# Expert rows scattered plainly into a table and fetched twice near the end, instead of accumulated into the token rows by DMA

## The reference

```python
def moe_swiglu(h, w_router, w1, w3, w2):
    logits = (h @ w_router).astype(jnp.float32)
    top_val, top_idx = lax.top_k(logits, TOP_K)          # TOP_K = 2
    top_w = jax.nn.softmax(top_val, axis=-1)
    combine = jnp.sum(jax.nn.one_hot(top_idx, N_EXPERTS, dtype=jnp.float32) * top_w[..., None], axis=-2)
    out = jnp.zeros_like(h)
    for e in range(N_EXPERTS):
        out = out + combine[..., e:e + 1].astype(h.dtype) * swiglu(h, w1[e], w3[e], w2[e])
    return out
...
x = x + moe_swiglu(h, moe_router[i], moe_w1[i], moe_w3[i], moe_w2[i])
...
return rms_norm(x, final_g)
```

## Time and profile before

| | us |
|---|---|
| median of 3 runs | 1800.87 (1799.14 to 1803.2) |
| the profiled execution | 1802.62 |
| its span, first to last instruction | 1800.9 |

### The profile page before, as it was taken

One profiled execution on the slowest core, in us unless ns is written; L12 is line 12 of the kernel. 1 busy time (PEld: TensorE's weight loads), 2 busy tenths in 40 slices (PEclk: granted clock), 3 DMA queues, 4 the chain that ended last, 5 costly groups with the idle time before them and its releaser, 6 DMA issues.

```text
span 1800.9 us, 24793 instructions
## 1 busy us (share of the span) xinstructions
PE 1778.0 (99%) x10058; PEld 1525.1 (85%) x10058; DVE 1507.2 (84%) x1402; ACT 1207.6 (67%) x1135; POOL 85.8 (5%) x97
## 2 busy tenths in 40 slices
PE   9999999999999999999999999999999999999997
PEld 9989898899999989898888887877878777787775
DVE  7999866566557999876579898999989899998997
ACT  5657754454445557654576787878878787787785
POOL 1000000100001000000100001001010010000000
PEclk9999999999999999999999999999999999999999
DMA  8444555345554544454468999999999999999995
GB/s 342 180 172 142 186 187 187 118 164 210 186 182 158 193 177 141 169 223 169 154 229 315 417 427 407 426 427 420 427 402 428 425 423 421 406 426 425 416 415 222
DMA packets 55826, 519.87 MB, mean 289 GB/s; under 512 B 7136, under 2 KB 7392, under 8 KB 12320
## 3 DMA queue, kind: packets, MB, share of 16 engines
q1 hardware_dynamic: 52448, 507.83, 70.7%
q0 software_dynamic: 2544, 9.18, 1.7%
q10 hardware_dynamic: 720, 1.31, 0.2%
HBM read 511.74 MB, written 6.55 MB: 288 GB/s over the span
## 4 chain that ended last, share of the span: by engine, by line
PE 84%; DVE 10%; ACT 4%; issue 2%; DMA 1%; SPq 0%; ACTq 0%; DVEq 0%
PE psum L2140 15%; PE psum L2126 13%; PE psum L2128 13%; PE psum L2127 13%; PE psum L2141 8%; PE psum L2634 7%; PE psum L2635 7%; DVE raw_alias L1374 3%; DVE U_alias L1374 2%; DVE wlo L1374 2%; ACT whi L832 1%; PE psum L2647 1%; PE psum L2629 1%; PE psum L2653 1%; ACT wlo L832 1%
## 5 line engine op out<-in xcount | busy, mean ns | idle before, releaser
L832 ACT ACTIVATE whi<-raw 128x2048 fp32r<-128x2048 f32 (+1 forms) x225 | 424.0, 1896 | 68.9 <-PE psum L2141 50.0
L1374 DVE TENSOR_TENSOR wlo<-raw,whi 128x2048 fp32r<-128x2048 f32 (+1 forms) x144 | 326.3, 2267 | 131.6 <-ACT whi L832 131.3
L2140 PE MATMUL psum<-h_hl,whi 128*128 128x512 f32 x1216 | 430.6, 398 | 0.3 <-DVE U L1732 0.2
L2141 PE MATMUL psum<-h_hl,wlo 128*128 128x256 f32 x1216 | 340.4, 280 | 0.0
L2140 PEld LDWEIGHTS psum<-h_hl,whi 128*128 128x128 f32 x1216 | 228.2, 188 | 55.4 <-issue 1.2
L2141 PEld LDWEIGHTS psum<-h_hl,wlo 128*128 128x128 f32 x1216 | 229.5, 189 | 0.1
L1374 DVE TENSOR_TENSOR raw_alias<-raw,wlo 128x2048 fp32r<-128x2048 f32 x87 | 196.5, 2284 | 18.4 <-ACT wlo L832 18.2
L2126 PE MATMUL psum<-act_hl,whi 128*128 128x256 f32 x720 | 206.1, 286 | 0.9 <-DVE wlo L1374 0.5
L2127 PE MATMUL psum<-act_hl,whi 128*128 128x256 f32 x720 | 203.7, 283 | 0.0
L2128 PE MATMUL psum<-act_hl,wlo 128*128 128x256 f32 x720 | 203.6, 283 | 0.0
L1374 DVE TENSOR_TENSOR raw_alias<-raw,whi 128x2048 fp32r<-128x2048 f32 x81 | 183.4, 2285 | 13.6 <-ACT whi L832 13.5
(11 more groups left out here) (335 smaller groups left out, 3379.4 us busy)
## 6 DMA issues: line engine op xcount, KB each, us to landing
raw<-in_stream SPq DMA_DIRECT2D x87, 2048.0 KB, 15.5
raw<-in_stream SPq DMA_DIRECT2D x141, 1024.0 KB, 4.8
U<-in_stream SPq DMA_DIRECT2D x52, 2048.0 KB, 14.2
memhat<-in_stream SPq DMA_DIRECT2D x29, 1024.0 KB, 11.1
h_hl_alias<-in_stream SPq DMA_DIRECT2D x29, 1024.0 KB, 13.1
raw<-in_stream SPq DMA_DIRECT2D x6, 512.0 KB, 3.7
xacc<-U POOLq DMA_DIRECT2D x3, 512.0 KB, 8.0
xT<-in_x_cols ACTq DMA_DIRECT2D x4, 256.0 KB, 6.9
```

Of the source, the lines that this page charges most:

```text
L832: act.activation(hi_home(n)[:, first:words], src[:, first:words], ACT.Copy).then_inc(hi_ready, 1)
L1374: dve.tensor_tensor(lo_home(n)[:, first:words], src[:, first:words], hi_home(n)[:, first:words].bitcast(F32), ALU.subtract).then_inc(lo_re ...
L2140: pe.matmul(o[:].rearrange("p (a b) -> p a b", a=2), st[0], mv, start=start, stop=False)
L2141: return pe.matmul(o[:, 0:256], st[1], mv[:, 0, :], start=False, stop=stop)
```

## The change

- `xacc` is replaced by `ys`: a row of zeros and 128 rows for each of the first 7 experts. Each expert's rows are stored into their own place by a plain scatter, with no addition. Rows of empty slots are dropped by a bounds check (an index beyond the table), in the scatters and in the gathers of tokens.
- `ys` is filled once, by 7 DMAs that ACT issues in layer 1 beside chunks 30 to 36 of its mixer and one for the zero row.
- DVE makes a list of where each token's two rows lie (`rows_listed`, at n = 16), as a larger and a smaller index. POOL fetches the rows of the smaller index into `xa` ahead of the scatter of p = 6, and those of the larger index into `xsum` after it.
- The residual: `xrows` and `x_rows` leave the opening steps, and the stores `kept` with them. PE transposes only the first block of tokens, after step 53, and DVE adds it to `xa` at n = 325 and 326. The second block is added by PE itself into the final sums, by 4 matmuls of `xT` with the identity in each of `final_rows(2)` and `(3)`.
- DVE adds `xsum` to `xa` in four pieces: at n = 333, 334, 335, and after the last split. `final_rows` wait for that; they move behind `turned(STEPS - 1)` and between the last down parts.
- A few expert's tokens are fetched as half rows on all 128 partitions.
- The shares are read in place (`wslot`), without the copy to `wcur`.

The diff, cut to its core:

```diff
@@ gpsimd
-            gp.iota(spare, ...)
-            gp.iota(minus_spare, ...)
+            gp.iota(row_of, pattern=[[SLOTS, NE]], base=1 + FAR, channel_multiplier=1, ...)
+            gp.memset(half_of, float(2 * S)).then_inc(rt_const, 1)
...
-            def kept(t):
-                gp.wait_ge(xt_ready, 2 * t + 2)
-                gp.dma_start(xacc[P * t:P * t + P, :], xtok).then_inc(scr_in, 16)
-            kept(0)
             gp.wait_ge(ix_ready, 1)
...
-                gp.indirect_dma_start(out=hg[0:there, :], out_offset=None, in_=hrow,
-                                      in_offset=bass.IndirectOffsetOnAxis(ap=gidx[0:there, p:p + 1], axis=0))\
-                  .then_inc(hg_in, 16)
-            for e in range(NE):
-                if e:
+                if few(p):
+                    out, rows, last = hg[:, 0:D // 2], hrow.rearrange("s (h d) -> (s h) d", h=2), 2 * S - 1
+                else:
+                    out, rows, last = hg, hrow, S - 1
+                gp.indirect_dma_start(out=out, out_offset=None, in_=rows,
+                                      in_offset=bass.IndirectOffsetOnAxis(ap=gidx[:, p:p + 1], axis=0),
+                                      bounds_check=last, oob_is_err=False).then_inc(hg_in, 16)
+            def sums_in(to, first):
+                for b in range(TB):
+                    at = first + b
+                    gp.indirect_dma_start(out=to[:, b, :], out_offset=None, in_=ys,
+                                          in_offset=bass.IndirectOffsetOnAxis(ap=yidx[:, at:at + 1], axis=0)).then_inc(xa_in, 16)
+            rows_in(1)
+            rows_in(2)
+            gp.wait_ge(scr_in, 16 * NE)
+            for e in range(NE - 1):
+                if e == NE - 2:
                     gp.wait_ge(y_sent, sent(e))
-                gp.tensor_copy(wcur, wslot[:, e:e + 1]).then_inc(wc_ready, 1)
...
-                    gp.indirect_dma_start(out=xacc, ..., in_=y[0:here, :], in_offset=None, compute_op=ALU.add)
-            gp.wait_ge(ga_done, NE)
-            gp.dma_start(xa, xacc[0:S, :].rearrange("(b p) d -> p b d", p=P)).then_inc(xa_in, 16)
+                    gp.wait_ge(ga_done, NE)
+                    sums_in(xa, TB)
+                here = HALF if few(e) else SLOTS
+                gp.wait_ge(y_ev, e + 2)
+                gp.indirect_dma_start(out=ys, ..., in_=y[0:here, :], in_offset=None,
+                                      bounds_check=(NE - 1) * SLOTS, oob_is_err=False).then_inc(y_sent, 16)
+                if e + 3 < NE:
+                    rows_in(e + 3)
+            gp.wait_ge(y_sent, sent(NE - 1))
+            sums_in(xsum, 0)
@@ scalar
+                    p = n - BASE[1] - CLEARED          # CLEARED = 30
+                    if 0 <= p < NE - 1:
+                        act.dma_start(ys[1 + SLOTS * p:1 + SLOTS * p + SLOTS, :].rearrange("p (a b) -> p a b", a=DB),
+                                      ones[:].unsqueeze(1).to_broadcast([P, DB, P])).then_inc(scr_in, 16)
...
             token_rows()
-            x_rows(0)
+            act.wait_ge(y_ev, 1)
+            act.dma_start(ys[0:1, :], y[0:1, :]).then_inc(scr_in, 16)
...
                 act.wait_ge(w_used, MOE + down_end(ENDS[p]) + 1)
-                act.wait_ge(wc_ready, p + 1)
+                if p:
+                    act.wait_ge(y_sent, sent(p))
...
                 for n in range(SPLIT, TOTAL):
-                    if n in (9, 15, 27):
-                        x_rows({9: 1, 15: 2, 27: 3}[n])
...
-                act.wait_ge(wc_ready, NE)
+                act.wait_ge(xa_sum, TB + 2)
@@ vector
+            def rows_listed():
+                ... (5 elementwise instructions and 2 reductions of 14 numbers per partition, a difference, a copy)
+            def kept_added(i):
+                t, at = i // 2, slice(512 * (i % 2), 512 * (i % 2) + 512)
+                if i == 0:
+                    dve.wait_ge(xa_in, 16 * TB)
+                dve.wait_ge(xt_done, i + 1)
+                dve.tensor_tensor(xa[:, t, at], bank[4 + i][:], xa[:, t, at], ALU.add).then_inc(xt_ready, 1)
+            def halves_added(i):
+                t, at = i // 2, slice(512 * (i % 2), 512 * (i % 2) + 512)
+                dve.wait_ge(xa_in, 32 * TB)
+                dve.wait_ge(xt_ready, 2)
+                dve.tensor_tensor(xa[:, t, at], xsum[:, t, at], xa[:, t, at], ALU.add).then_inc(xa_sum, 1)
...
-                routing = {..., 14: shares_placed, 21: places}
+                routing = {..., 14: shares_placed, 16: rows_listed, 21: places}
...
+                    if n in (325, 326):
+                        kept_added(n - 325)
+                    if n in (333, 334, 335):
+                        halves_added((2, 3, 0)[n - 333])
...
+                halves_added(1)
@@ tensor
-            xrows(0)
...
-                elif f in (1, 2, 4):
-                    k = {1: 1, 2: 2, 4: 3}[f]
-                    pe.wait_ge(xt_ready, k)
-                    xrows(k)
...
                 def final_rows(i):
+                    pe.wait_ge(xa_sum, (2, 3, 0, 1).index(i) + 1)
                     pe.matmul(final_bank(0, i // 2, i % 2), ident[:], xa[:, i // 2, at:at + 512], ...)
+                    if i > 1:
+                        for k in range(4):
+                            c = 4 * (i % 2) + k
+                            pe.matmul(final_bank(0, 1, i % 2)[:, P * k:P * k + P], xT[:, c, P:S], ident[:], ...)
...
                     if last:
                         folded_gate(s)
-                        pe.wait_ge(xa_in, 16)
-                        pe.wait_ge(st_ready, 1)
-                        for i in (2, 3):
-                            final_rows(i)
...
+                    if s == STEPS - 3:
+                        pe.wait_ge(y_ev, NE)
+                        for i in range(TB):
+                            xrows(i)
                 down_part(STEPS - 2, 0)
                 turned(STEPS - 1)
+                final_rows(2)
+                down_part(STEPS - 2, 1)
+                final_rows(3)
                 final_rows(0)
-                down_part(STEPS - 2, 1)
+                down_part(STEPS - 1, 0)
                 final_rows(1)
-                for half in range(2):
-                    down_part(STEPS - 1, half)
+                down_part(STEPS - 1, 1)
```

More of the change, by code:

```diff
@@ L323, in trunk @@
         comb = facts[:, :, 2:2 + NE]
-        spare, minus_spare = rt[:, 645:646], rt[:, 646:647]
-        wslot, wcur = rt[:, 648:656], rt[:, 656:657]
-        place = rt[:, 664:672]
+        row_of = rt[:, 664:672]
+        wslot = rt[:, 648:656]
+        rows_f = rt[:, 644:648]
+        half_of = rt[:, 656:657]
         gidx, sidx = sb("gidx", [P, NE], U32), sb("sidx", [P, NE], U32)
         idxu = sb("idxu", [P, TB, NE], U32)
+        yidx = sb("yidx", [P, 2 * TB], U32)
         wts = rt[:, 592:608]
@@ L335, in trunk @@
         he_hi, he_lo = v(2048, D), v(3072, D)
+        act_plain = aliased("act_hl", F32)
+        xsum = act_plain[:, 2048:4096].rearrange("p (b d) -> p b d", b=TB)
         h_plain = aliased("h_hl", F32)
@@ L1208, in rows_out @@
                     at = slice(512 * k, 512 * k + 512)
-                    ins = act.activation(y[0:rows, at], bank[y_bank(p) + k][0:rows, :], ACT.Copy, scale=wcur[0:rows, :])
+                    ins = act.activation(y[0:rows, at], bank[y_bank(p) + k][0:rows, :], ACT.Copy,
+                                         scale=wslot[0:rows, p:p + 1])
                     if few(p):
@@ L1318, in last_rows @@
                     return
-                act.wait_ge(wc_ready, NE)
+                act.wait_ge(xa_sum, TB + 2)
                 for half in range(2):
                     act.wait_ge(*((w_used, MOE + NE * PER_E) if half else (y_first, 1)))
-                    act.activation(y_hi[:, 512 * half:512 * half + 512], bank[y_bank(NE - 1) + half][:], ACT.Copy, scale=wcur)\
+                    act.activation(y_hi[:, 512 * half:512 * half + 512], bank[y_bank(NE - 1) + half][:], ACT.Copy,
+                                   scale=wslot[:, NE - 1:NE])\
                        .then_inc(y_hi_s, 1)
@@ L1328, in kept_rows @@
                 act.wait_ge(y_lo_s, 1)
-                act.activation(y[:, 0:512], bank[y_bank(NE - 1)][:], ACT.Copy, scale=wcur).then_inc(y_ev, 1)
+                act.wait_ge(y_sent, sent(NE - 1))
+                act.activation(y[:, 0:512], bank[y_bank(NE - 1)][:], ACT.Copy, scale=wslot[:, NE - 1:NE]).then_inc(y_ev, 1)
             def finish(r):
@@ L1986, in first_round @@
                     gathered(1, k, 0, bank[2 + k][:])
-                routing = {5: ranked, 6: listed, 7: counted, 8: placed, 13: shares, 14: shares_placed, 21: places}
+                routing = {5: ranked, 6: listed, 7: counted, 8: placed, 13: shares, 14: shares_placed, 16: rows_listed, 21: places}
                 for n in range(SPLIT, TOTAL):
@@ L2681, in brought @@
             def brought(p, k, to):
-                rows = HALF if few(p) else SLOTS
                 pe.wait_ge(hg_in, 16 * p)
```

(8 more changed lines are left out.)

97 lines of the change are left out of this document (51 added, 46 removed).

## The result

The kernel after took 1805.8 us (median of 20 runs, 1803.35 to 1808.95), the kernel before 1800.93 (20 runs, 1798.44 to 1804.43). The ratio is 1.0027, 95% interval 1.0021 to 1.0033, so 3.8 to 5.9 us slower. A later comparison gave 1.0026 (1.0015 to 1.0037). The forecast was 1804.6 us, +3.7.

The account below looks back on a forecast made before the run. PE was taken to bound the body and the last run, DVE the opening's start and the stretch to 1770. Opening -0.5 and end +4.2 gave +3.7 us: 1804.6 us against the median 1800.87, range 1797.0 to 1808.5.

Parts of the forecast that it names:

- What bounds the kernel: Path: PE from 962 to 1734, ACT once, DVE to 1770, PE to 1789, then 11.6 us of normalisation and output.
- Opening: Residual transposes leave the opening; only the fourth group, at 990.41, lies where PE is the pace: gain 0.5 us.
- `rows_listed`: Opening, DVE at n = 16: 8 tiny instructions, about 1.9 us, covered with 1 us to spare; taken as 0, bounds 0 and +1.9.
- The first few expert's rows: Opening: fetched 2 us sooner, as half rows landing at 991.2 against a need at 990.1; taken as 0, bounds 0 and +1.1.
- Filling `ys`: Trunk: 7 issues on ACT, 1 us allowed for each, PE waits for nothing there; taken as 0, bounds 0 and +7.
- DMA relief: Body: lighter memory traffic, 7 us of stream for four scatter pairs, priced at 0 as PE waited for no landing.
- rival 1: Body: the memory stream is the bound and gives back the whole relief, -8 us, so 1796.6 in all; chance 15%.
- The end on DVE: Two `kept_added` before splits 325 and 326, 0.65 each: PE starts its last run 1.3 us later, at 1771.6.
- The end on PE: PE waits 1.1 for split 332, then moved `final_rows` 1.7 and residual matmuls 1.8: ends at 1793.5, 4.2 us later.
- Covers at the end: `halves_added` end near 1787.5, before PE needs the last near 1790; the `xsum` fetch lands by 1767, asked for at 1779.
- Rival 3: Near 1748: two `xsum` gather issues on POOL stop DVE's gapless run, +2 to +3 us more, 1807.1; chance 8%.

## Why the prediction was right

*What bounds the kernel.* Right. PE in the body, DVE from the last `rows_out` to about 1770, PE behind it. The plain scatters and the segments of the table show the body blind to a lighter stream.

*Opening, -0.5.* Right, by the right group: 0.46 in the run without `xrows`. In after, without the clock losses of 3.4 and 1.7, it is 133.0 us (960.90 to 1097.33) against 133.6: -0.5. The two profiles show -0.38 at the mark of p = 0 by chance: after's has no fall of the clock at 910 to 916, where before's loses 1.7 us, and a longer one at 968.

*`rows_listed`, about 1.9 us, covered.* Covered, with the size too high: from 962.87 to the product at 964.15 it is 1.3 us. Its eight operations have 14 columns or fewer; of the four from 930.42 on from which I took the price, three have 64. The cover is what I had named; with six lists, PE waited 4.5 us.

*The first few expert's rows.* Right with 0. POOL issues the fetch at 977.72 instead of 979.77, and PE goes from L2654 at 990.04 to the transposes at 990.57 without a wait.

*Filling `ys`.* Right with 0: no step of the trunk is longer. One of DVE's last instructions of the trunk, which waits for PE's result, starts at 905.55 against 905.48.

*DMA relief, 0.* Right, and rival 1 is wrong: a good part of the relief is there (3.4 us of stream lacking around the scatters for 10.8, ACT's waits of 5.6 us gone) and it returns 0.1 us at most. The argument, no wait of PE leads to a landing, held for taking load away. I used it for adding load too, in what I expected of the doubled scatters, and there it fails: they cost 10.7 us.

*The end on DVE, +1.3.* It is 1.15 by the start of PE's last run (34.04 us behind the mark, against 32.89) and 1.19 in the run without the adds. The pitch is 0.60, not 0.65.

*The end on PE.* PE was forecast at split 332 at 1778.1, released at 1779.2, its end at 1793.5. It came at 1778.06, went on at 1779.06, and began its last product at 1793.23. That 1778.1 was hit so closely is luck in part: PE began its last run 0.3 us sooner than forecast and came to the down parts 0.2 faster, and then took 4.18 us for 16 products instead of 3.65. The moved rows (2 x 0.86) and the float32 matmuls (0.81 + 0.89) are the forecast 1.7 and 1.8. The term was 4.2 and is 4.35.

*Covers at the end.* `halves_added` ended at 1787.3, forecast 1787.5; PE took the last of them at 1789.96 without a wait. The second fetch was issued at 1745.46 and 1747.61, landed about 13.7 us later, near 1761, and was asked for at 1778.92.

*Rival 3, DVE held by POOL.* It did not come: DVE is busy for 20.00 of 20 us around the two fetch issues, as around the one copy before. No run here shows DVE held by POOL; of the rule (the Trainium skill, "SBUF — State Buffer", "Who interferes with whom") the trace bears out at most the half in which POOL waits.

*What the sum left out.* -0.5 + 0.2 (body) + 4.35 = +4.0, the runs say +4.7 to +4.9. So 0.7 to 0.9 us of the loss are outside of the sum, and the number came out inside its range in spite of them. I had no term for the clock, although stand right beside a stretch in which it falls. The change takes `xrows` out of PE's work ahead of the small matmuls there. The clock is the best candidate for the rest, by the table of the clock; the clocks of whole runs give 0.2 to 0.5 us of it. It isn't shown, and the rest stays open.

## What to carry to other kernels

Before adding work near the end, ask in each stretch which engine is the pace, and put the work where it is another one: the same sums, with the order that they forced on PE, cost 4.35 us in the last run of PE and on DVE's gapless stretch, and nothing 10 to 30 us earlier on POOL's queue, ACT and in PE's slack. Moving work out of a gap has a price though nothing is added: the gap comes back as a wait, and the work is done behind it (1.37 us here for 1.7 us of moved work). The stream here, hidden but by the estimate at 96% of its time, gave nothing when it was relieved and took 10.7 us when it was loaded, a part of it by way of PE's clock. So test both sides before calling a resource free.

## What the runs showed of the hardware

- A row of small matmuls is dear beyond its own time: behind 32 of 128x10 (3.6 us at the full clock), or before their end, PE's clock fell to 0.50 in 10 of the 12 profiles that have them in one row, and cost 1.7 or 3.4 us. The one with the long wait is among them; there it fell during the wait, and cost 5.7. Cut in two, 1.8 us each with a chunk's products between, it did not fall in either of two. The clock also fell at 910 to 920, around the start of the experts, in 5 of the 14 profiles, for 1.7 or 3.4 us. Two profiles of one kernel differ by 1.7 us in it (before, and the small matmuls in two halves), while the times of one kernel spread over 6; how much of the spread it makes was not measured.
- PE's clock also fell when PE waited: to 0.50 during the 4.5 us wait with six lists, and during or behind waits of 2.7 and 2.5 us with doubled scatters, for 3.4 and 1.7 us.
- A fetch that adds to what lies in SBUF as it lands took 13.0 us (median of the four fetches of that kernel, one of them plain), no more than the plain ones, 13.4 and 13.7. An accumulating scatter to memory took 11.2 us, a plain one 9.9.
- A small DVE operation on 14 columns takes 0.17 us, and the next one starts 0.20 us after its start where the program makes it wait for the one before, and 0.08 where it doesn't.
